# Head 0 of a hybrid decoder layer: a later load of head 2, keys ahead of values, and an earlier key product

## What is computed

```
def forget_attend(q, cq, qpos, k, v, ck, kpos):
    s = jnp.einsum('bqhd,bkhd->bhqk', q, k).astype(jnp.float32) * ATT_SCALE
    s = s + jnp.swapaxes(cq, 1, 2)[:, :, :, None] - jnp.swapaxes(ck, 1, 2)[:, :, None, :]
    s = jnp.where(kpos[None, :] <= qpos[:, None], s, -jnp.inf)
    p = jax.nn.softmax(s, axis=-1)
    return jnp.einsum('bhqk,bkhd->bqhd', p.astype(v.dtype), v)
...
x = x + merged @ lp['w_out']
```

## Time and profile before

| | before |
|---|---|
| median of three runs | 3105.7 us |
| profiled execution, its own time | 3101.6 us |
| its span, first to last instruction | 3099.9 us |
| mean granted TensorE clock | 0.977 of full |
| TensorE busy | 2937.8 us, 95% |
| round 0 of the attention | about 675 to 782 us |
| rounds 1 to 6 | about 75 us each |

### The profile page before, as it was taken

One profiled execution on the slowest core, in us unless ns is written; L12 is line 12 of the kernel. 1 busy time (PEld: TensorE's weight loads), 2 busy tenths in 40 slices (PEclk: granted clock), 3 DMA queues, 4 the chain that ended last, 5 costly groups with the idle time before them and its releaser, 6 DMA issues.

```text
span 3099.9 us, 44526 instructions
## 1 busy us (share of the span) xinstructions
PE 2937.8 (95%) x15733; PEld 2590.6 (84%) x15733; DVE 1366.3 (44%) x1885; ACT 758.8 (24%) x1529; POOL 1220.3 (39%) x595
## 2 busy tenths in 40 slices
PE   4999999986999999889999999999999999999998
PEld 4899999853555555479999999999999999999998
DVE  5312344466777776151255544554454462221221
ACT  7000333332333333340110000000000013443442
POOL 1111111187777776057642222222222224444453
PEclk8999999978999999989999999999999999999999
DMA  7222333467888887444521111111111125555553
GB/s 226 73 75 85 113 115 108 120 193 229 272 268 266 271 268 229 133 157 146 166 86 55 45 46 45 55 42 41 53 45 46 45 91 175 178 196 176 183 198 107
DMA packets 247895, 420.37 MB, mean 136 GB/s; under 512 B 44574, under 2 KB 152299, under 8 KB 243235
## 3 DMA queue, kind: packets, MB, share of 16 engines
q1 hardware_dynamic: 166994, 321.56, 32.7%
q10 hardware_dynamic: 80472, 96.01, 9.2%
q0 software_dynamic: 288, 1.05, 0.1%
HBM read 335.13 MB, written 83.46 MB: 135 GB/s over the span
## 4 chain that ended last, share of the span: by engine, by line
PE 45%; POOL 2%; DVE 1%; DMA 1%; ACT 1%; issue 1%; SPq 0%; DVEq 0%; ACTq 0%; POOLq 0%
PE PS L2600 32%; PE PS L2688 4%; PE PS L2690 4%; PE PS L2689 4%; DVE YT L2199 1%; POOL DL L1118 1%; ACT DH L1545 0%; DMA GRb<-gT 0%; DMA GRa<-gT 0%; PE PS L2672 0%; DMA out_y_prompt<-YT 0%; POOL ML L1067 0%; DVE GL L2181 0%; POOL R L1078 0%; DMA DR<-in_w_down 0%
## 5 line engine op out<-in xcount | busy, mean ns | idle before, releaser
L2600 PE MATMUL PS<-MH,VS 128*128 128x416 f32 (+1 forms) x4000 | 1081.9, 351 | 4.8 <-issue 3.2
L2600 PEld LDWEIGHTS PS<-MH,VS 128*128 128x128 f32 x4000 | 750.5, 188 | 14.8 <-issue 4.6
L2600 PE MATMUL PS<-ML,VS 128*128 128x416 f32 (+1 forms) x2000 | 700.7, 350 | 0.0
L2600 PEld LDWEIGHTS PS<-ML,VS 128*128 128x128 f32 x2000 | 376.7, 188 | 2.6 <-issue 0.8
L1118 POOL TENSOR_TENSOR DL<-DR,DH 128x1408 fp32r<-128x1408 f32 x80 | 258.5, 3231 | 289.5 <-ACT DH L1545 289.4
L2688 PE MATMUL PS<-GH,DH 128*128 128x416 f32 (+1 forms) x880 | 315.4, 358 | 17.3 <-DVE GL L2181 8.9
L1047 POOL CAST VS<-VR 128x1024 fp32r<-128x1024 f32 x52 | 57.9, 1114 | 693.0 <-PE PS L2600 691.2
L963 POOL TENSOR_TENSOR prod<-Kpg,qb 128x1024 f32<-128x1024 f32 x128 | 304.4, 2378 | 53.3 <-POOL prod L963 27.6
L2484 PE MATMUL PS<-PT,VA 128*65 128x416 f32 (+16 forms) x816 | 310.5, 463 | 3.9 <-ACT PT L1408 3.0
L2690 PE MATMUL PS<-GH,DL 128*128 128x416 f32 (+1 forms) x880 | 310.9, 353 | 0.0
L2689 PE MATMUL PS<-GL,DH 128*128 128x416 f32 (+1 forms) x880 | 309.6, 352 | 0.0
(11 more groups left out here) (295 smaller groups left out, 4262.2 us busy)
## 6 DMA issues: line engine op xcount, KB each, us to landing
Kpg<-in_cache_k SPq DMA_DIRECT2D x256, 256.0 KB, 4.2
Vpg<-in_cache_v SPq DMA_DIRECT2D x256, 256.0 KB, 4.7
DR<-in_w_down SPq DMA_DIRECT2D x80, 704.0 KB, 4.1
gT<-GO ACTq DMA_DIRECT2D x110, 208.0 KB, 1.9
VR<-in_w_up SPq DMA_DIRECT2D x44, 512.0 KB, 3.4
GRb<-gT SPq DMA_DIRECT2D x31, 416.0 KB, 5.2
WR<-in_w_stream SPq DMA_DIRECT2D x21, 512.0 KB, 3.5
GRa<-gT SPq DMA_DIRECT2D x24, 416.0 KB, 5.6
```

The costliest lines, as they stand in the source:

```text
L2600: mm = e.matmul(PS[:, j, 0:full(j)], w[:, u, k], x[:, k, j * BW:j * BW + full(j)], start=(k == 0 and q == 0), stop=(k == KC - 1 and q == 2))
```

## The change

It moves steps of round 0 and touches no arithmetic. The new-key product (two VectorE instructions) leaves `scores_end` and becomes a step of its own, `new key`, at tile 9 for sample 0 and at tile 46 for sample 1 of round 0 (in rounds 1 to 6 it stays directly ahead of `end`). Sample 0's `turn` to `weight sum` move two tiles on (`turn` from 16 to 18; `end` stays at 15). `pages` of round 0 move to tiles 26, 30, 33, 36, 40, 43, 46 and 50. SyncE issues sample 1's key groups 0 to 3 ahead of sample 0's value groups 0 to 3. In the round's queue the loads of head 2 move from place 23 to 37.5 and those of sample 2's query from 31 to 34.

```
-    plan[22 if first else 4].append(("weight sum", 0))
+    plan[24 if first else 4].append(("weight sum", 0))
...
-                plan[23 + 27 * g // 15].append(("pages", g // 2))
+                plan[25 + 25 * g // 15].append(("pages", g // 2))
...
-        for t, step in ((15, "end"), (16, "turn"), (17, "top"), (18, "spread max"), (19, "less"), (20, "exps"), (21, "sums")):
+        for t, step in ((9, "new key"), (15, "end"), (18, "turn"), (19, "top"), (20, "spread max"), (21, "less"), (22, "exps"), (23, "sums")):
...
-        for t, step in ((47, "end"), (48, "turn"), (48, "top"), (49, "spread max"), (49, "less"), (49, "exps"),
+        for t, step in ((47, "end"), (46, "new key"), (48, "turn"), (48, "top"), (49, "spread max"), (49, "less"), (49, "exps"),
...
-        at = 23 + 27 * (2 * b + 1) // 15 if first else 5 + (37 if last else 43) * (2 * b + 1) // 15
+        at = 25 + 25 * (2 * b + 1) // 15 if first else 5 + (37 if last else 43) * (2 * b + 1) // 15
...
-    found += [(20, "values", 0), (23, "head", 0), (31, "query", 0)] if first else \
+    found += [(20, "values", 0), (34, "query", 0), (37.5, "head", 0)] if first else \
...
+            for g in range(4):
+                fetch_keys(1, g)
             e.wait_ge(lf_tp, 16)
             e.wait_ge(c_att, 2)
             for g in range(4):
                 fetch_cached_values(0, g)
-            for g in range(4):
-                fetch_keys(1, g)
...
+            def new_key(s, v):
+
+                e.wait_ge(nw_ld, 32 * s + 32)
+                if s == 0:
+                    e.wait_ge(c_att2, 7)
+                e.tensor_tensor(knb[:, v], knb[:, v], qb[0:1, v], ALU.mult).then_inc(kp, 1)
+                e.wait_ge(kp, s + 1)
+                e.tensor_reduce(scw[0:1, v, 0, :], knb[:, v].rearrange("p (h d) -> p h d", d=HD), AX.X, ALU.add).then_inc(kf, 1)
```

More of the change, by code:

```diff
@@ L190, in attention_plan @@
     if first:
-        for t, step in ((15, "end"), (16, "turn"), (17, "top"), (18, "spread max"), (19, "less"), (20, "exps"), (21, "sums")):
+        for t, step in ((9, "new key"), (15, "end"), (18, "turn"), (19, "top"), (20, "spread max"), (21, "less"), (22, "exps"), (23, "sums")):
             plan[t].append((step, 0))
     if not last:
-        for t, step in ((47, "end"), (48, "turn"), (48, "top"), (49, "spread max"), (49, "less"), (49, "exps"),
+        for t, step in ((47, "end"), (46, "new key"), (48, "turn"), (48, "top"), (49, "spread max"), (49, "less"), (49, "exps"),
                         (50, "sums")) if first else \
-                ((36, "end"), (42, "turn"), (43, "top"), (44, "spread max"), (45, "less"), (46, "exps"), (48, "sums")):
+                ((36, "new key"), (36, "end"), (42, "turn"), (43, "top"), (44, "spread max"), (45, "less"), (46, "exps"), (48, "sums")):
             plan[t].append((step, 1))
@@ L1915, in scores_end @@
                     e.wait_ge(lf_ev, 16)
[L1916 to L1919, removed]
                 e.wait_ge(kf, 4 * s + 2)
@@ L1980, in dve_head @@
                             page_scores(i + n // 16, (u + n // 16) % 2, n % 16)
+                        if what == "new key":
+                            new_key(i + n, v)
                         if what == "end":
```

## The result

The kernel after takes 3109.89 us (median of 20 runs, 3105.6 to 3117.53), the kernel before, run beside it, 3105.06 us (20 runs). The ratio is 1.0021, 95% interval 1.0014 to 1.0028: slower by 4.8 us as the medians stand and by 6.5 us as the ratio does. That is about the 0.2% which the prediction took for the bound of what can be told from none, but the interval excludes 1. The forecast was 3109.7 us. In every ratio of this document the few executions that took over 1.5% longer than the fastest of their kernel are left out (four in all, of 3304.8 us and more), and the medians keep them. The profiled execution of after has its own time of 3110.76 us and a span of 3109.0 us.

A forecast was written before the change was run, and what follows sets the result against it. SyncE's queue was taken as the bound from 726 on. The terms 0 + 0 + 4.0 gave +4.0 us on the profiled 3101.6, so 3105.6; with the median 4.1 us above that execution, 3109.7, range 3102.5 to 3115.

The forecast's parts named there:

- The queue is the bound from 726 on: Round 0: SyncE's queue runs without a wait from 726.29 to value groups 14 and 15 at 771.79.
- Keys of sample 1 first: product 0 without a wait, the preparing 3.65 us sooner: GpSimd in round 0: product 0 starts at 692.9, it and head 1's preparing 3.65 us sooner; cost zero.
- All early gain goes into the wait at pages(2): TensorE in round 0: 7 to 9 us won by tile 26 are all lost waiting at pages(2).
- The turn's wait shrinks to at most 2.5 us, and its low clock probably goes: TensorE at sample 0's turn: the 5.38 us wait shrinks to at most 2.5; low clock, about 4.5 us lost, probably goes.
- pages(6) +4.0 us: Round 0: head 2's bytes ahead of value group 13 make pages(6) start at 778.3 instead of 774.28.
- pages(7) without a wait, the end follows pages(6): End of round 0: pages land at 783.9, TensorE comes at 785.8 without waiting; the round ends 4.0 us later.
- the rival of the clock: Low clock after the longer wait before pages(6) lasts 9 us, adding 4.3 us, 3114.0 in all; chance 0.13.
- The hidden bytes: Rival: head 2 flows at the pages' 376 GB/s, pages(6) starts at 774.2, no change, 3105.6; chance 0.20.
- The +0.2 us that the prediction worked out from a bound of 358 GB/s: Round 0's end by the skill's bound: head 2 takes 6.0 us, end moves +0.2 instead of +4.0; not taken.
- The won stalls: Rival: the removed 5.4 and 9.75 us waits of round 0 are time won, 3090.6; chance 0.07.
- the term "zero" of the keys-first swap: SyncE's queue in round 0: issuing sample 1's keys ahead of value groups 0 to 3 adds zero to the sum.

The follow-up runs named there:

- e2: The kernel before with only head 2's loads moved to place 37.5 of SyncE's queue; 3110.95 us, ratio to before 1.0019.
- e4: The kernel before with the changed kernel's whole queue order but the old engine plan (tile places); 3111.86 us, ratio to before 1.0013.
- e5: The kernel after with the second copies of head 2's queries and keys in round 0 cut to 16 columns; 3103.32 us, ratio to before 1.0001.
- e3: The kernel before with only sample 1's key groups 0 to 3 issued ahead of value groups 0 to 3; 3100.82 us, ratio to before 0.9982.
- e9: The same kernel as e3, run again unchanged; 3099.05 us, ratio to before 0.9984.
- e1: The kernel after with head 2's loads put back at place 23 of round 0's queue; 3106.48 us, ratio to before 0.9994.
- e8: The kernel before with the changed kernel's queue order, but head 2 left at place 23 and the old engine plan; 3105.58 us, ratio to before 1.0006.
- e11: The same kernel as e1, run again unchanged; 3108.28 us, ratio to before 1.0012.
- e12: The kernel after with each head's queries and keys loaded over 128 partitions by half the columns, in every round; 3342.13 us, ratio to before 1.0763.

## Why the prediction was right

By the steps of the prediction:

- *The queue is the bound from 726 on.* Right. Key group 8 went out 52.6 us into the round (forecast 727.9, 53.2), head 2 at 84.6 (forecast 758.8, 84.1). The stretch between them, 17 groups at 1.1 us, four readings of page numbers at 2.75 and the query, was 32.0 us where the sum gave 30.9.
- *Keys of sample 1 first: product 0 without a wait, the preparing 3.65 us sooner.* Right. That product starts 17.2 us into the round (694.75), with only the 0.29 us between two products ahead of it; the forecast's 692.9 is 18.2, before had 21.9. Product 4 starts at 47.2 (724.80) in place of 51.6, 4.4 us sooner. Counted from the span's start it is only 1.5 us sooner than before's 726.32; the 2.9 us of the round's start lie between the two counts. On the way GpSimd waited 1.86 us for VectorE, which the forecast did not have.
- *All early gain goes into the wait at pages(2).* Half right. pages(2) came 5.0 us sooner (forecast 4.9, at 738) and the gain went no further, but the wait was 6.9 us and not 10 or more, since the early gain was small: TensorE was ready for pages(2) at 56.6 into the round and not at 58.8, one tile further on, where I had 7 to 9 us by tile 26. What my walk left out is the next wait: at pages(5) 5.3 us, where before had 1.3. I had said that the same walk brings pages(3) to pages(5) forward; pages(5) came forward by 0.7.
- *The turn's wait shrinks to at most 2.5 us, and its low clock probably goes.* The wait: right, with 2.55 us one step on, at the spread of the maximum. The low clock: wrong. It is 0.82 over 703 to 712 where it was 0.50 only because it starts later: by stretches of 1 us it is low from 708.8 to 715.7, 6.8 us, where before had 10.2 (702.4 to 712.6). That is probably one reason for the small early gain.
- *pages(6) +4.0 us.* The mechanism is shown (e2, e4 and e5): head 2's bytes stand ahead of value groups 12 and 13. The term was mis-sized: +5.4 in the round. One count needs no start of a round: from product 4 to pages(6) are 57.8 us (724.80 to 782.58), before 48.0, and the forecast had 55.6 (722.7 to 778.3). The missing 2.2 us are 1.1 in the queue between key group 8 and head 2 and 0.9 behind head 2; the rest is small. Head 2 went out 0.5 us later in the round than forecast, and from its issue to the landing of group 13's last page were 20.3 us (771.8 + 10.6 - 762.14) instead of 19.4. Round 1 had 20.8, from which I had taken 1.4 for the store.
- *pages(7) without a wait, the end follows pages(6).* Right, with 0.76 us more under the low clock: 777.1 to 787.3, 10.2 us long. That is the rival of the clock, but small (0.76 us of its 4.3 between these two steps). Its premise came true, for the low stretch is 6.8 us longer than before's 3.4, but 5.5 us of it (to 782.58) passed while TensorE stood waiting, with no work to slow. The round is 6.2 us longer in these two profiles; the medians say 4.8.
- *The hidden bytes (0.20)* fell: the rate was 229 GB/s in full traffic too. The +0.2 us that the prediction worked out from a bound of 358 GB/s fell with it: the head load flowed far below that bound, and the pages, at 387, above it. *The won stalls (0.07)* fell: the stalls were removed and the next ones took their place.

What the sum hid: the term "zero" of the keys-first swap was the net of two. By itself the swap brings about 5 us (e3, e9), since the whole queue moves forward; the new order of keys and values behind it takes that back (e1, e8 and e11 against e3 and e9); and the late head costs 2.6 us on top by the medians and 5.6 by the ratios (after against the mean of e1 and e11), 5.5 us in e2. My walk had the first two in it (1.24 us from the earlier start against 3.85 for one more group and reading) and gave only their outcome. The number was right; the reader of it could not have seen that one part of the change was worth keeping. And that it came within 0.2 us of the median is luck: the effect itself was put at 4.0 us and measured 4.8 or 6.5, and the base of 3105.7 us was 0.6 us above the median of the 20 runs beside after.

## What to carry over

When an in-order queue is the bound, a removed wait is worth what it brings forward **the last transfer that something waits for**, so walk the queue to that one, with its issue costs and with its bytes. A bulk load moved from an idle stretch of the DMA engines to a full one delays what stands behind it by its transfer time, however late its own consumer is: here half of head 2's bytes, 4.9 us, made the pages behind 4.9 us late. And try the parts of a change by themselves: of the four parts here (keys first, order, late head, plan) one was a gain that two others hid.

## What the runs showed that I had not expected

- **Loads of different shape ran at very different rates, with all engines busy.** Head loads over 64 partitions moved 219 to 229 GB/s at a DMA share of 1.01 to 1.02, page loads over 128 partitions 376 to 387 at 1.05, so the share does not tell them apart; with a source pattern of 2 x 64 rows, 52 GB/s on two engines' share. The Trainium skill (SBUF — State Buffer, section Door 1: The DMA port swizzle) states that partitions 0 to 63 reach only 8 of 16 ports, with an asymptote of about 218 GB/s; the trace agrees with its number, at 219, and lies 5% above it at 229. No run here tests the mechanism, since e12 ran into the other effect first.
- **VectorE's wide elementwise step and GpSimd's products hold each other up.** The scale of all scores took 1.75 us before and 0.41 us after, for the same 128 x 264 elements. Timelines of VectorE and of GpSimd, first of before, then of after:

```profile
700.20 1.75 DVE L1921 SCALAR_TENSOR_TENSOR scw<-scw,cb 128x264 f32<-128x264 f32 x1
```

```profile
699.21 2.45 POOL L963 TENSOR_TENSOR prod<-Kpg,qb 128x1024 f32<-128x1024 f32 x1 [0.29 <-POOL prod L963]
701.95 2.35 POOL L963 TENSOR_TENSOR prod<-Kpg,qb 128x1024 f32<-128x1024 f32 x1 [0.29 <-POOL prod L963]
```

```profile
702.81 0.41 DVE L1926 SCALAR_TENSOR_TENSOR scw<-scw,cb 128x264 f32<-128x264 f32 x1
```

```profile
702.83 2.62 POOL L963 TENSOR_TENSOR prod<-Kpg,qb 128x1024 f32<-128x1024 f32 x1 [0.29 <-POOL prod L963]
```

In before the scale begins within a product and ends in the gap behind it, at 701.95. After's begins as a product has ended (the gap is 702.54 to 702.83) and is done at once, and the product that follows takes 2.62 us in place of 2.36. The new key's sum, a reduction with one input, took 0.67 us in both. Round 7 of before has the counter-test: GpSimd has done its last product at 1221.53, and the new-key product, 1.92 us in the earlier trace rows, takes 0.67, and the scale 0.43. The other seven times the scale took 1.75 to 1.79. VectorE in round 7:

```profile
1225.23 0.67 DVE L1917 TENSOR_TENSOR knb<-knb,qb 1x512 f32<-1x512 f32 x1
...
1226.65 0.43 DVE L1921 SCALAR_TENSOR_TENSOR scw<-scw,cb 128x264 f32<-128x264 f32 x1
```

The Trainium skill (SBUF — State Buffer, section Who interferes with whom) states that a VectorE instruction with two inputs in SBUF contends with a GpSimd instruction that reads SBUF; these rows agree, for the scale and the new-key product have two, and the sum has one.
- **GpSimd's products can wait for VectorE's sums.** After a long low-clock stretch of TensorE at the round's start, VectorE's sums, which come with TensorE's tiles, are late, and GpSimd stands: 1.86 us in after, 4.53 in e1 (timeline of e1), none in e3. The low stretch ends at 681.5 in after, 687.3 in e1 and 675.3 in e3. It is probably a part of the scatter of single executions; no run tests that.

```profile
692.02 2.37 POOL L963 TENSOR_TENSOR prod<-Kpg,qb 128x1024 f32<-128x1024 f32 x1 [4.53 <-DVE scw L1884]
```
